# Modulation matmuls of the delta rounds: one weight block of three summed on VectorE

## The chip, the cores and the metric

One core of a Trainium2 chip. The metric is device time of one execution in microseconds (us), the median over runs. All data are float32.

## What is computed

The program is two layers of models behind each other on 256 tokens of width 1024. The first block normalizes the tokens, projects them, runs a short convolution, a gated delta rule (8 heads, both directions), a state-space mixer (SSD), an output projection and an expert layer. The second block runs two attention layers. Each of these scales, shifts and gates its tokens by a modulation vector, which depends on one conditioning row `c` alone:

```python
c_act = jax.nn.silu(c)                        # 1 x 1024
for l in range(DEPTH_2):                      # 2 layers
    mod = c_act @ w_ada[l] + b_ada[l]         # (1 x 1024) @ (1024 x 3072)
    shift, scale, gate = split_cols(mod, (D, D, D))
```

`w_ada` is 2 x 1024 x 3072 floats, 25 MB. It is independent of the tokens, so the kernel computes it while the delta rule runs.

## The kernel before, in words

The kernel is written engine by engine; each engine runs its own list of instructions in the order written, and semaphores order the engines (`Steps` counts named steps of one semaphore, `X.at("name", r)` is its count at that step in round r).

**Weights.** All large weights come through a ring in SBUF, in blocks of 2 MB, in the order of `stream_plan`. The SP queue issues each load as soon as the block that last held the slot has been read. Up to the expert layer only two slots are in use, taken in turn (`n % 2`). The 12 blocks of `w_ada_2` are 1024 x 512: eight row groups k of 128 rows on the partitions, 512 columns each. TensorE takes a block with `take`, and `block_read` puts its release on the next matmul that TensorE issues, whichever it is.

**The delta stage** has four rounds r, two heads (s = 0, 1) in each. A round finishes the inverse of a triangular matrix by block steps and then runs the recurrence. In TensorE's order: P5 (matmuls of `LT` with the operands `Xf` that GpSimd builds), X5 and Y5 (they need G5, the masked P5 that VectorE makes in `masked`), P6, Y6 (needs G6), then the state products u, S, K2, Q2, u2, o. Each is 8 matmul records a head of 128x128 (X5 with Y5 16). VectorE also copies Y5's result to `Y`, ScalarE copies X5's. GpSimd builds the next round's `Xf` and `Yf` as soon as P5 and Y5 of this round no longer read them (four instructions, line 2627).

**The modulation** rides in the same rounds, three blocks n = 3r, 3r+1, 3r+2 each, in two steps:

- `ada_rows(n)`, the row pass: for each k, `ccol[:, k]` (silu of c, 128 values) as weights, widened to 32 columns, and the 128x512 rows of the block as moving operand. Four column strips of bank 6 take k = 0..3 and then k = 4..7 on top, so the bank ends with four partial rows, each in 32 copies. ScalarE (`rows_out`) copies the bank to `ntmp`.
- `ada_cols(n)`: four matmuls with 128x128 pieces of `ntmp` as weights and a column of 1/32 (`one32`) as moving operand; they sum over the partitions and leave the 512 results as four columns in bank 7. VectorE (`ada_out`) copies them to `modc`.

The order in a round before: rows 3r, P5, cols 3r, rows 3r+1, X5 and Y5, cols 3r+1, rows 3r+2, P6, Y6, cols 3r+2, and then the recurrence. Bank 6 is one buffer, so `ada_rows` waits for the ScalarE copy of the block before; bank 7 also, so `ada_cols` waits for VectorE's copy before it.

**Round 0** starts when the gate projection is done and GpSimd has built the first operands from the inverse, which came back through DRAM.

Of the kernel before, what the change touches and what calls it, by code (L numbers as in the profile page):

```python
# [7 lines left out]
P = 128  # L8
F32 = mybir.dt.float32
F32R = mybir.dt.float32r  # L10
ALU = mybir.AluOpType
ACT = mybir.ActivationFunctionType
# [6 lines left out]
DK = D // P  # L19
# [161 lines left out]
def hybrid_kernel(nc, A, out, scratch):  # L181
# [7 lines left out]
    with ctx:  # L189
        def sem(name):  # L190
            return ctx.enter_context(nc.semaphore(name))
# [36 lines left out]
        with ExitStack() as st:  # L228
# [64 lines left out]
            xw = [cT[:, KT0 + 2 * i:KT0 + 2 * i + 2, :].rearrange("p a n -> p (a n)") for i in range(4)]  # L293
            hst = [free[:, (24 + 4 * i) * P:(28 + 4 * i) * P] for i in range(2)]
            yint = late
            onat = knat
            ynat = vnat
            mixT = cT[:, 0:MT, :]
# [181 lines left out]
        ssds_pe = Steps(sem("ssds_pe"), "h y")  # L480
        ssds_pool = Steps(sem("ssds_pool"), "xw")
        ssds_act = Steps(sem("ssds_act"), "h")
        ada_pe = Steps(sem("ada_pe"), "rows cols")
        ada_act = Steps(sem("ada_act"), "rows")
        ada_dve = Steps(sem("ada_dve"), "cols")
        c_ready = sem("c_ready")
        mix_act = Steps(sem("mix_act"), "gdn ssd")
        mix_gdn, mix_ssd = Steps(sem("mix_gdn"), "pair"), Steps(sem("mix_ssd"), "mixed")
        delta_norm = sem("delta_norm")
# [150 lines left out]
        def _(pe):  # L640
# [44 lines left out]
            def mm(o, lhsT, rhs, start=True, stop=True):  # L685
                return release(nc.tensor.matmul(o, lhsT, rhs, start=start, stop=stop))  # L686
# [152 lines left out]
            def ada_rows(n, r):  # L839


                w = take("w_ada_2")
                if n == 0:
                    pe.wait_ge(c_ready, 2)
                if n % 3 == 0 and r:
                    for s in range(2):
                        pe.wait_ge(gdn_act[s].sem, gdn_act[s].at("Q2", r - 1))
                if n:
                    pe.wait_ge(ada_act.sem, n)
                for k in range(DK):  # L850
                    j = k % 4
                    last = mm(bank[6][32 * j:32 * j + 32, :], ccol[:, k:k + 1].to_broadcast([P, 32]), w[:, k, :], k < 4, k >= 4)
                last.then_inc(ada_pe.sem, ada_pe.one("rows"))
                block_read()

            def ada_cols(n):

                pe.wait_ge(ada_act.sem, n + 1)
                if n:
                    pe.wait_ge(ada_dve.sem, n)  # L860
                for i in range(4):
                    last = mm(bank[7][:, i:i + 1], ntmp[:, n % 2, i * P:(i + 1) * P], one32[:])
                last.then_inc(ada_pe.sem, ada_pe.one("cols"))

            def ssd_args(u):

# [10 lines left out]

            pe.wait_ge(lt_pool.sem, GH)
            for r in range(GH // 2):
                ada_rows(3 * r, r)  # L880
                for s in range(2):
                    h = 2 * r + s
                    p_, d_, a_ = gdn_pe[s], gdn_dve[s], gdn_act[s]
# [3 lines left out]
                    for i in range(4):  # L887
                        last = mm(q4(A_[s], i), LT[:, h, i, :], Xf[s][:, i, :])
                    last.then_inc(p_.sem, p_.one("P5"))
                ada_cols(3 * r)  # L890
                ada_rows(3 * r + 1, r)
                for s in range(2):
                    p_, d_, a_ = gdn_pe[s], gdn_dve[s], gdn_act[s]
                    pe.wait_ge(d_.sem, d_.at("G5", r))
                    for i in range(4):
                        last = mm(q4(B_[s], i), Yf[s][:, i, :], G[s][:, i, :])
                    last.then_inc(p_.sem, p_.one("X5"))
                    for i in range(4):
                        last = mm(q4(C_[s], i), G[s][:, i, :], Yf[s][:, i, :])
                    last.then_inc(p_.sem, p_.one("Y5"))  # L900
                ada_cols(3 * r + 1)
                ada_rows(3 * r + 2, r)
                for s in range(2):
# [594 lines left out]
        def _(act):  # L1498
# [8 lines left out]
            def f(o, i, fn, scale=1.0, bias=0.0, **kw):  # L1507
                return nc.scalar.activation(o, i, fn, scale=scale, bias=bias, **kw)  # L1508
# [125 lines left out]
            for r in range(GH // 2):  # L1634
                if r:
                    delta_squares(r - 1)
                def each():
                    for s in range(2):
                        yield s, 2 * r + s, gdn_pe[s], gdn_dve[s], gdn_act[s], gdn_pool[s]
                def rows_out(n):  # L1640
                    act.wait_ge(ada_pe.sem, ada_pe.at("rows", n))
                    f(ntmp[:, n % 2, :], bank[6][:], ACT.Copy).then_inc(ada_act.sem, ada_act.one("rows"))
                rows_out(3 * r)
                rows_out(3 * r + 1)
                for s, h, p_, d_, a_, o_ in each():
                    act.wait_ge(p_.sem, p_.at("X5", r))
                    f(X[s], bank[1 + 3 * s][:].rearrange("p (i n) -> p i n", i=4), ACT.Copy).then_inc(a_.sem, a_.one("X5"))
                rows_out(3 * r + 2)
                for s, h, p_, d_, a_, o_ in each():
                    act.wait_ge(p_.sem, p_.at("Y6", r))  # L1650
                    f(Y[s], bank[2 + 3 * s][:].rearrange("p (i n) -> p i n", i=4), ACT.Copy).then_inc(a_.sem, a_.one("Y6"))
                for s, h, p_, d_, a_, o_ in each():
                    act.wait_ge(d_.sem, d_.at("us", r))
                    f(U[s][:, 0:2, :], bank[6 + s][:, 0:2 * P].rearrange("p (i n) -> p i n", i=2), ACT.Copy
                      ).then_inc(a_.sem, a_.one("u"))
                for s, h, p_, d_, a_, o_ in each():
                    act.wait_ge(p_.sem, p_.at("S", r))
                    f(LT[:, h, 2:4, :], bank[3 * s][:, 0:2 * P].rearrange("p (i n) -> p i n", i=2), ACT.Copy
                      ).then_inc(a_.sem, a_.one("S"))
                for s, h, p_, d_, a_, o_ in each():  # L1660
                    act.wait_ge(p_.sem, p_.at("Q2", r))
                    for i, (c, d) in enumerate(((1, 0), (0, 1))):
                        last = f(QS[s][:, c, :], bank[6 + s][:, i * P:(i + 1) * P], ACT.Copy,
                                 scale=eg[:, c, d * GH + h:d * GH + h + 1])
                    last.then_inc(a_.sem, a_.one("Q2"))
# [314 lines left out]
        def _(dve):  # L1980
# [153 lines left out]
            for r in range(GH // 2):  # L2134
# [4 lines left out]
                    return tt(G[s].rearrange("p (c d) n -> p c (d n)", c=TT), bank[3 * s][:].rearrange("p (c n) -> p c n", c=TT),  # L2139
                              gmask[b].rearrange("p d n -> p (d n)").unsqueeze(1).to_broadcast([P, TT, 2 * P]), ALU.mult)  # L2140
                def ada_out(n):
                    dve.wait_ge(ada_pe.sem, ada_pe.at("cols", n))
                    nc.vector.tensor_copy(modc[:, 4 * n:4 * n + 4], bank[7][:, 0:4]).then_inc(ada_dve.sem, ada_dve.one("cols"))
                for s, h, p_, d_, a_, o_ in each():
                    dve.wait_ge(p_.sem, p_.at("P5", r))
                    masked(s, 5).then_inc(d_.sem, d_.one("G5"))
                ada_out(3 * r)
                for s, h, p_, d_, a_, o_ in each():
                    dve.wait_ge(p_.sem, p_.at("Y5", r))
                    nc.vector.tensor_copy(Y[s], bank[2 + 3 * s][:].rearrange("p (i n) -> p i n", i=4)).then_inc(d_.sem, d_.one("Y5"))  # L2150
                ada_out(3 * r + 1)
                for s, h, p_, d_, a_, o_ in each():
                    dve.wait_ge(p_.sem, p_.at("P6", r))
# [582 lines left out]
```

## Time and profile before

| | |
|---|---|
| median of 3 runs | 1373.17 us (1367.18 to 1374.37) |
| the profiled execution | 1375.73 us |
| its span | 1373.7 us |
| TensorE busy | 1226.6 us (89% of the span) |
| TensorE weight loads, beside it | 926.1 us (67%) |
| VectorE busy | 645.5 us (47%) |
| ScalarE busy | 410.6 us (30%) |
| GpSimd busy | 331.0 us (24%) |

The span is what the profiler saw from the first instruction to the last; the execution's own time is a little longer. A float32 matmul appears as two records. Where an engine is busy 89% over the whole, single stages may still wait for something else, so the shares say little on one stage. The delta stage runs from about 253 to 364 us of the span. "Granted clock" is the share of 2.4 GHz that TensorE was given: 1.00 is 2.4 GHz, 0.50 would be 1.2 GHz, and a value between is a stretch with some of both.

### The profile page before, as it was taken

How to read it: one execution, taken by the hardware profiler on the slowest of the kernel's cores; microseconds unless marked ns; L12 is line 12 of the kernel's file. 1: busy time of each engine (PE TensorE's matmuls, PEld its weight loads, DVE VectorE, ACT ScalarE, POOL GpSimd, SP SyncE). 2: the span in 40 equal slices, each digit the busy share in tenths (PEclk: the TensorE clock that was granted, in tenths of full speed). 3: DMA queues.
4: the chain of work that ended last, by engine and by line, in shares of the span. 5: the costliest groups of instructions: out<-in, count | busy, mean ns of one | idle time of the engine just before them, and what ended most of it. 6: DMA issues, size and time to landing. Idle time of an engine off the chain costs nothing.

```text
span 1373.7 us, 17987 instructions
## 1 busy us (share of the span) xinstructions
PE 1226.6 (89%) x7446; PEld 926.1 (67%) x7446; DVE 645.5 (47%) x1059; ACT 410.6 (30%) x991; POOL 331.0 (24%) x322
## 2 busy tenths in 40 slices
PE   6989789899999699978789998998988999899887
PEld 5878655577754332212129797998878889798777
DVE  1597758133560300001026355575887245466785
ACT  4345542133631410100014521311524441230332
POOL 0386640412200300000021122132253112223231
PEclk9999989999999799999999999999999999999999
DMA  5333333766406699999982435153332245335310
GB/s 196 123 123 123 123 92 134 267 242 218 152 30 275 257 386 421 422 421 422 421 340 71 160 107 204 62 173 134 123 111 85 96 172 170 114 114 184 123 62 31
DMA packets 91554, 257.02 MB, mean 187 GB/s; under 512 B 7645, under 2 KB 12534, under 8 KB 79058
## 3 DMA queue, kind: packets, MB, share of 16 engines
q1 hardware_dynamic: 89122, 248.67, 48.3%
q0 software_dynamic: 2032, 6.95, 1.6%
q8 instruction: 58, 0.95, 0.3%
q10 hardware_dynamic: 320, 0.26, 0.1%
q14 instruction: 22, 0.18, 0.0%
HBM read 253.49 MB, written 2.12 MB: 186 GB/s over the span
## 4 chain that ended last, share of the span: by engine, by line
PE 63%; DMA 14%; DVE 9%; ACT 7%; POOL 5%; issue 2%; SPq 0%; DVEq 0%; ACTq 0%; POOLq 0%
PE bank L686 59%; DMA ring<-in_w_up_dram 8%; DMA ring<-in_w_down_dram 4%; PE bank L695 3%; DVE ring_r L1993 3%; POOL late L2595 3%; POOL acc L2596 2%; DVE acc L2064 2%; ACT ring L1508 1%; DMA ring<-in_w_ada_dram 1%; ACT cT L1508 1%; ACT L1508 1%; ACT oa L1508 1%; ACT qkT L1508 1%; ACT xT L1508 0%
## 5 line engine op out<-in xcount | busy, mean ns | idle before, releaser
L2698 POOL CAST w_hi_r<-ring 128x1024 fp32r<-128x1024 f32 x136 | 151.0, 1138 | 670.4 <-DMA ring<-in_w_in_dram 267.3
L686 PE MATMUL bank<-ring_r,xT_hi 128*128 128x256 f32 (+1 forms) x864 | 245.9, 285 | 0.0
L686 PE MATMUL bank<-w_hi_r,xT_hi 128*128 128x256 f32 x704 | 208.6, 296 | 24.2 <-DVE ring_r L1993 19.8
L686 PE MATMUL bank<-w_hi_r,xT_r 128*128 128x256 f32 x704 | 202.6, 288 | 0.0
L1993 DVE TENSOR_TENSOR ring_r<-ring,w_hi_r 128x1024 fp32r<-128x1024 f32 x136 | 182.6, 1375 | 41.9 <-POOL w_hi_r L2698 41.9
L686 PEld LDWEIGHTS bank<-ring_r,xT_hi 128*128 128x128 f32 x864 | 168.3, 195 | 0.2
L686 PEld LDWEIGHTS bank<-w_hi_r,xT_hi 128*128 128x128 f32 x704 | 137.2, 195 | 36.5 <-DVE ring_r L1993 25.7
L686 PEld LDWEIGHTS bank<-w_hi_r,xT_r 128*128 128x128 f32 x704 | 136.9, 195 | 0.0
L686 PE MATMUL bank<-ring,xsT 128*32 128x512 f32 x496 | 111.8, 595 | 26.4 <-DMA ring<-in_w_up_dram 13.2
L686 PE MATMUL bank<-xT,ring 128*128 128x256 f32 x576 | 127.5, 384 | 0.0
L686 PEld LDWEIGHTS bank<-xT,ring 128*128 128x128 f32 x576 | 111.0, 193 | 15.3
L2064 DVE SCALAR_TENSOR_TENSOR acc<-raw,cols,acc 128x256 f32<-128x256 f32 x168 | 99.3, 600 | 24.2 <-ACT acc L1508 19.3
L686 PEld LDWEIGHTS bank<-ring,xsT 128*32 128x32 f32 x496 | 28.0, 110 | 105.5 <-issue 65.3
L686 PE MATMUL bank<-ring,cT 128*128 128x512 f32 (+1 forms) x224 | 67.7, 460 | 2.8 <-ACT cT L1508 2.8
L2595 POOL TENSOR_SCALAR late<-raw,cols 128x256 f32<-128x256 f32 x48 | 48.6, 1012 | 83.2 <-ACT acc L1508 79.3
L2326 DVE TENSOR_TENSOR hid<-hid,bank 128x512 f32<-128x512 f32 x4 | 2.8, 688 | 134.3 <-PE bank L686 134.3
L1508 ACT ACTIVATE prob<-prob,nmx 128x256 f32<-128x256 f32 x64 | 32.1, 503 | 101.8 <-DVE smx L2451 55.0
L686 PE MATMUL bank<-ring,hidT 128*32 128x512 f32 x256 | 54.7, 595 | 8.0 <-DMA ring<-in_w_down_dram 5.3
L2442 DVE TENSOR_TENSOR prob<-bank,bias 128x256 f32<-128x256 f32 x64 | 24.2, 420 | 77.0 <-PE bank L686 77.0
L1508 ACT ACT_TABLE_LOAD x45 | 57.7, 1283 | 8.5 <-DVE sz L2021 6.1
L686 PE MATMUL bank<-xT_hi,w_hi_r 128*128 128x256 f32 x208 | 59.2, 285 | 0.0
L686 PE MATMUL bank<-xT_hi,ring_r 128*128 128x256 f32 x208 | 58.8, 283 | 0.0
(360 smaller groups left out, 2133.0 us busy)
## 6 DMA issues: line engine op xcount, KB each, us to landing
ring<-in_w_in_dram SPq DMA_DIRECT2D x39, 2048.0 KB, 7.8
ring<-in_w_up_dram SPq DMA_DIRECT2D x32, 1024.0 KB, 16.3
ring<-in_w_down_dram SPq DMA_DIRECT2D x32, 1024.0 KB, 16.3
ring<-in_w_gate_dram SPq DMA_DIRECT2D x30, 1024.0 KB, 16.4
ring<-in_w_ada_dram SPq DMA_DIRECT2D x12, 2048.0 KB, 8.8
ring<-in_w_out_dram SPq DMA_DIRECT2D x8, 2048.0 KB, 7.7
ring<-in_w_o_mla_dram SPq DMA_DIRECT2D x2, 2048.0 KB, 12.6
ring<-in_w_o_swa_dram SPq DMA_DIRECT2D x2, 2048.0 KB, 7.8
```

The source lines that it names most:

```text
L686: return release(nc.tensor.matmul(o, lhsT, rhs, start=start, stop=stop))
L695: return release(nc.tensor.transpose(o, i, eye[0:i.shape[0], 0:i.shape[0]]))
L1508: return nc.scalar.activation(o, i, fn, scale=scale, bias=bias, **kw)
L1993: tt(lo, raw_, hi.bitcast(F32), ALU.subtract).then_inc(lo_done.sem, lo_done.one("piece"))
L2064: ins = stt(out=acc[:, n % 4, :], in0=raw[:, n % 4, j:j + T], scalar=tap(n, j), in1=acc[:, n % 4, :], op0=ALU.mult, op1=ALU.add)
L2326: tt(v, v, bank[1][:], ALU.mult).then_inc(ex_dve.sem, ex_dve.one("h"))
L2442: last = tt(prob[:, u % 2, m, :], bank[m][:, 0:T], bv[:, m, :], ALU.add)
L2595: link(nc.gpsimd.tensor_scalar(prod[:, j % 2], raw[:, n % 4, j:j + T], tap(n, j), None, ALU.mult))
L2596: ins = nc.gpsimd.tensor_tensor(acc[:, n % 4, :], acc[:, n % 4, :], prod[:, j % 2], ALU.add)
L2698: nc.gpsimd.tensor_copy(hi, raw_).then_inc(hi_done.sem, hi_done.one("piece"))
```

## The change

The middle block of each round, 3r+1, is no longer multiplied on TensorE. VectorE (`ada_block`) waits until it has landed and computes the sum over k of `w[:, k] * ccol[:, k]` with one tensor_scalar and seven scalar_tensor_tensor instructions of 128x512, each of which waits for the one before (`link`), into `asum` (a quarter of the `late` buffer). TensorE then sums `asum` over the partitions in `ada_cols(3r+1)`, with a column of ones from `tri`, and takes and releases the block only there. ScalarE's copy for that block is gone.

The order changes too. On TensorE: P5, rows 3r, X5 and Y5, cols 3r, cols 3r+1, rows 3r+2, P6, Y6, cols 3r+2. On VectorE: G5 of both heads, the block sum, both Y5 copies, the copies of cols 3r and 3r+1, G6. The one semaphore for rows and cols becomes two, and `rows_index` counts the remaining row passes.

```diff
@@ -293,6 +293,7 @@
             xw = [cT[:, KT0 + 2 * i:KT0 + 2 * i + 2, :].rearrange("p a n -> p (a n)") for i in range(4)]
             hst = [free[:, (24 + 4 * i) * P:(28 + 4 * i) * P] for i in range(2)]
             yint = late
+            asum = late[3]
             onat = knat
             ynat = vnat
             mixT = cT[:, 0:MT, :]
@@ -480,10 +481,17 @@
         ssds_pe = Steps(sem("ssds_pe"), "h y")
         ssds_pool = Steps(sem("ssds_pool"), "xw")
         ssds_act = Steps(sem("ssds_act"), "h")
-        ada_pe = Steps(sem("ada_pe"), "rows cols")
+        ada_rows_pe, ada_cols_pe = Steps(sem("ada_rows_pe"), "rows"), Steps(sem("ada_cols_pe"), "cols")
+        ada_sum = Steps(sem("ada_sum"), "block")
         ada_act = Steps(sem("ada_act"), "rows")
         ada_dve = Steps(sem("ada_dve"), "cols")
         c_ready = sem("c_ready")
+        n_ada = next(n for n, block in enumerate(plan) if block[0] == "w_ada_2")
+
+        def rows_index(n):
+
+            return n - (n + 1) // 3
+
         mix_act = Steps(sem("mix_act"), "gdn ssd")
         mix_gdn, mix_ssd = Steps(sem("mix_gdn"), "pair"), Steps(sem("mix_ssd"), "mixed")
         delta_norm = sem("delta_norm")
@@ -846,21 +854,29 @@
                     for s in range(2):
                         pe.wait_ge(gdn_act[s].sem, gdn_act[s].at("Q2", r - 1))
                 if n:
-                    pe.wait_ge(ada_act.sem, n)
+                    pe.wait_ge(ada_act.sem, rows_index(n))
                 for k in range(DK):
                     j = k % 4
                     last = mm(bank[6][32 * j:32 * j + 32, :], ccol[:, k:k + 1].to_broadcast([P, 32]), w[:, k, :], k < 4, k >= 4)
-                last.then_inc(ada_pe.sem, ada_pe.one("rows"))
+                last.then_inc(ada_rows_pe.sem, ada_rows_pe.one("rows"))
                 block_read()
 
             def ada_cols(n):
 
-                pe.wait_ge(ada_act.sem, n + 1)
                 if n:
                     pe.wait_ge(ada_dve.sem, n)
+                if n % 3 == 1:
+                    take("w_ada_2")
+                    pe.wait_ge(ada_sum.sem, n // 3 + 1)
+                    v, ones = asum, tri[:, 1, 0:1]
+                else:
+                    pe.wait_ge(ada_act.sem, rows_index(n) + 1)
+                    v, ones = ntmp[:, rows_index(n) % 2], one32[:]
                 for i in range(4):
-                    last = mm(bank[7][:, i:i + 1], ntmp[:, n % 2, i * P:(i + 1) * P], one32[:])
-                last.then_inc(ada_pe.sem, ada_pe.one("cols"))
+                    last = mm(bank[7][:, i:i + 1], v[:, i * P:(i + 1) * P], ones)
+                last.then_inc(ada_cols_pe.sem, ada_cols_pe.one("cols"))
+                if n % 3 == 1:
+                    block_read()
 
             def ssd_args(u):
 
@@ -877,7 +893,6 @@
 
             pe.wait_ge(lt_pool.sem, GH)
             for r in range(GH // 2):
-                ada_rows(3 * r, r)
                 for s in range(2):
                     h = 2 * r + s
                     p_, d_, a_ = gdn_pe[s], gdn_dve[s], gdn_act[s]
@@ -887,8 +902,7 @@
                     for i in range(4):
                         last = mm(q4(A_[s], i), LT[:, h, i, :], Xf[s][:, i, :])
                     last.then_inc(p_.sem, p_.one("P5"))
-                ada_cols(3 * r)
-                ada_rows(3 * r + 1, r)
+                ada_rows(3 * r, r)
                 for s in range(2):
                     p_, d_, a_ = gdn_pe[s], gdn_dve[s], gdn_act[s]
                     pe.wait_ge(d_.sem, d_.at("G5", r))
@@ -898,6 +912,7 @@
                     for i in range(4):
                         last = mm(q4(C_[s], i), G[s][:, i, :], Yf[s][:, i, :])
                     last.then_inc(p_.sem, p_.one("Y5"))
+                ada_cols(3 * r)
                 ada_cols(3 * r + 1)
                 ada_rows(3 * r + 2, r)
                 for s in range(2):
@@ -1638,10 +1653,9 @@
                     for s in range(2):
                         yield s, 2 * r + s, gdn_pe[s], gdn_dve[s], gdn_act[s], gdn_pool[s]
                 def rows_out(n):
-                    act.wait_ge(ada_pe.sem, ada_pe.at("rows", n))
-                    f(ntmp[:, n % 2, :], bank[6][:], ACT.Copy).then_inc(ada_act.sem, ada_act.one("rows"))
+                    act.wait_ge(ada_rows_pe.sem, rows_index(n) + 1)
+                    f(ntmp[:, rows_index(n) % 2, :], bank[6][:], ACT.Copy).then_inc(ada_act.sem, ada_act.one("rows"))
                 rows_out(3 * r)
-                rows_out(3 * r + 1)
                 for s, h, p_, d_, a_, o_ in each():
                     act.wait_ge(p_.sem, p_.at("X5", r))
                     f(X[s], bank[1 + 3 * s][:].rearrange("p (i n) -> p i n", i=4), ACT.Copy).then_inc(a_.sem, a_.one("X5"))
@@ -2139,15 +2153,29 @@
                     return tt(G[s].rearrange("p (c d) n -> p c (d n)", c=TT), bank[3 * s][:].rearrange("p (c n) -> p c n", c=TT),
                               gmask[b].rearrange("p d n -> p (d n)").unsqueeze(1).to_broadcast([P, TT, 2 * P]), ALU.mult)
                 def ada_out(n):
-                    dve.wait_ge(ada_pe.sem, ada_pe.at("cols", n))
+                    dve.wait_ge(ada_cols_pe.sem, n + 1)
                     nc.vector.tensor_copy(modc[:, 4 * n:4 * n + 4], bank[7][:, 0:4]).then_inc(ada_dve.sem, ada_dve.one("cols"))
+                def ada_block(n):
+                    dve.wait_ge(landed[slot[n_ada + n]], arrived(n_ada + n))
+                    dve.wait_ge(c_ready, 2)
+                    w = ring[slot[n_ada + n]][:].rearrange("p (k n) -> p k n", k=DK)
+                    for k in range(DK):
+                        if k:
+                            ins = stt(out=asum, in0=w[:, k], scalar=ccol[:, k:k + 1], in1=asum, op0=ALU.mult, op1=ALU.add)
+                        else:
+                            ins = ts(asum, w[:, k], ccol[:, k:k + 1], None, ALU.mult)
+                        if k < DK - 1:
+                            link(ins)
+                    ins.then_inc(ada_sum.sem, ada_sum.one("block"))
+
                 for s, h, p_, d_, a_, o_ in each():
                     dve.wait_ge(p_.sem, p_.at("P5", r))
                     masked(s, 5).then_inc(d_.sem, d_.one("G5"))
-                ada_out(3 * r)
+                ada_block(3 * r + 1)
                 for s, h, p_, d_, a_, o_ in each():
                     dve.wait_ge(p_.sem, p_.at("Y5", r))
                     nc.vector.tensor_copy(Y[s], bank[2 + 3 * s][:].rearrange("p (i n) -> p i n", i=4)).then_inc(d_.sem, d_.one("Y5"))
+                ada_out(3 * r)
                 ada_out(3 * r + 1)
                 for s, h, p_, d_, a_, o_ in each():
                     dve.wait_ge(p_.sem, p_.at("P6", r))
```

## Rows read from the trace of the kernel before

**Rows 1.** Chain that ended last, shares of the span by engine.

```profile
PE 63%; DMA 14%; DVE 9%; ACT 7%; POOL 5%; issue 2%; SPq 0%; DVEq 0%; ACTq 0%; POOLq 0%
```

**Rows 2.** Stretches: length, busy PE, PEld, DVE, ACT, POOL; clock, DMA share, GB/s.

```profile
253.00:279.00 26.00, 21.03 (x162) 15.56 (x163) 6.59 (x15) 4.74 (x9) 9.93 (x8) 0.93 0.88 311
279.00:304.00 25.00, 24.57 (x208) 19.64 (x207) 8.01 (x19) 8.00 (x23) 5.03 (x4) 1.00 0.67 239
```

**Rows 3.** Chain in order of time, its transfers of 225 to 400 us.

```profile
254.57 7.78 DMA ring<-in_w_ada_dram
...
338.75 8.78 DMA ring<-in_w_ada_dram
```

**Rows 4.** Timeline of round 1, TensorE: start, length, instruction, count.

```profile
285.05 1.92 PE L686 MATMUL bank<-ring,ccol 128*32 128x512 f32 x16
...
286.90 2.05 PE L686 MATMUL bank<-ring 128*128 128x128 f32 x16
...
288.79 0.95 PE L686 MATMUL bank<-one,ntmp 128*128 128x1 f32 x8
...
291.52 3.84 PE L686 MATMUL bank<-ring 128*128 128x128 f32 x32
...
297.93 3.99 PE L686 MATMUL bank<-cT,ring 128*128 128x128 f32 x32
```

**Rows 5.** The same timeline, VectorE: last sum of round 0, G5, Y5 copy.

```profile
285.15 0.42 DVE L2176 TENSOR_TENSOR w_hi<-bank,ring 128x256 f32<-128x256 f32 x1 [0.47 <-PE bank L686]
...
288.99 0.69 DVE L2139 TENSOR_TENSOR ring<-bank,tri 128x512 f32<-128x512 f32 x1 [0.20 <-PE bank L686]
...
293.61 0.69 DVE L2150 COPY cT<-bank 128x512 f32<-128x512 f32 x1 [3.67 <-PE bank L686]
```

**Rows 6.** VectorE by line (ns min/median/max), and the convolution from 52 us.

```profile
L2565 DVE SCALAR_TENSOR_TENSOR xres<-tmp,stat,xres x4: 745/748/752, 1035.5 to 1359.0; 128x512 f32<-128x512 f32 x4
...
L1997 DVE CAST xT_hi<-xT 128x512 fp32r<-128x512 f32 x8 | 3.4, 425 | 7.1 <-ACT xT L1508 7.1
...
L2064 DVE SCALAR_TENSOR_TENSOR acc<-raw,cols,acc x168: 470/486/1011, 52.1 to 181.5; 128x256 f32<-128x256 f32 x168
...
52.06 5.91 DVE L2064 SCALAR_TENSOR_TENSOR acc<-raw,cols,acc 128x256 f32<-128x256 f32 x9
...
52.00:58.00 6.00, 6.00 (x29) 5.29 (x28) 5.72 (x10) 1.79 (x4) 5.45 (x7) 1.00 0.34 102
```

**Rows 7.** Timeline: GpSimd in round 1, GpSimd and VectorE from 363 us.

```profile
293.66 3.75 POOL L2627 TENSOR_TENSOR ring<-cT,tri 128x512 f32<-128x512 f32 x3 [4.24 <-PE bank L686]
...
363.52 4.62 POOL L2647 TENSOR_TENSOR w_hi<-xnat,drow 128x1024 f32<-128x1024 f32 x2 [3.57 <-DVE w_hi L2176]
...
365.41 0.97 DVE L2210 TENSOR_TENSOR cT<-cT 128x512 f32<-128x512 f32 x1 [1.33 <-ACT cT L1508]
...
367.47 1.22 DVE L2192 TENSOR_TENSOR ring<-ring 128x512 f32<-128x512 f32 x1 [1.09 <-ACT ring L1508]
```

**Rows 8.** Load of block 5: its issue, and KB with us to landing.

```profile
287.42 0.37 SPq L621 DMA_DIRECT2D ring<-in_w_ada_dram  x1
...
ring<-in_w_ada_dram SPq DMA_DIRECT2D x1, 2048.0 KB, 7.9
```

**Rows 9.** Round 0: TensorE's timeline, and the stretch 262 to 265.

```profile
253.52 1.92 PE L686 MATMUL bank<-ring,ccol 128*32 128x512 f32 x16 [0.84 <-issue]
...
256.70 1.16 PE L686 MATMUL bank<-ring 128*128 128x128 f32 x8 [1.25 <-POOL ring L2627]
...
259.16 1.16 PE L686 MATMUL bank<-ring 128*128 128x128 f32 x8 [1.30 <-POOL ring L2627]
...
264.80 4.89 PE L686 MATMUL bank<-ring 128*128 128x128 f32 x32
...
272.26 4.00 PE L686 MATMUL bank<-cT,ring 128*128 128x128 f32 x32
...
262.00:265.00 3.00, 2.61 (x17) 0.62 (x18) 0.00 (x0) 0.09 (x1) 0.00 (x0) 0.77 1.05 388
```

## The prediction, made before the changed kernel was run

> **What bounds the kernel now.** I read the page first. The chain that ended last is TensorE for 63% and transfers for 14% [rows 1], so work taken from another engine is worth nothing unless TensorE waits for it. Then I cut the delta stage into its rounds. From the second round on TensorE is busy 24.57 of 25 us at full clock, VectorE only 8.01 [rows 2]: the stage is TensorE's instruction order, one round every 25.67 us (P6 starts at 272.26 in round 0 and at 297.93 in round 1) [rows 4, 9]. In round 0 it is not: TensorE is busy 21.03 of 26 us at clock 0.93. The chain of waits adds one thing [rows 3]: two transfers of modulation blocks are on it, 7.78 us in round 0 and 8.78 us in round 3. So the third block of a round lands about when TensorE wants it: the two-slot ring has next to no slack today, which a moved release will show.
>
> **One round in TensorE's order** [rows 4], offsets from 285.05: row pass of block 3 at 0.0, P5 1.85, column sums 3.74, row pass of block 4 4.62, X5 and Y5 6.47, column sums 10.15, row pass of block 5 11.03, P6 12.88 (of the row passes and column sums, which repeat, the first stands in the rows). Back to back, a row pass takes 1.85 us, column sums 0.88, P5 1.85, X5 with Y5 3.68. VectorE's mask G5 of the second head ends 2.78 us after P5 starts (288.99 + 0.69 against 286.90) [rows 4, 5].
>
> **What the change removes.** One row pass a round, 1.85 us of TensorE, and one ScalarE copy, which lay beside TensorE's work and was worth nothing. Without new waits P6 would start at 11.0 instead of 12.88. Moving the other row pass behind P5 costs nothing by itself in rounds 1 to 3: P5 then needs bank 0 and 3 free, and VectorE's last sum of the round before starts at 285.15 and takes 0.42 us [rows 5], done while the first head's P5 (about 1 us) runs.
>
> **What it adds on VectorE.** One tensor_scalar and seven scalar_tensor_tensor, 128x512, chained. The row with the same form (a per-partition scalar, both tensors in SBUF) is 748 ns; the one-source op of that size, a cast, 425 ns [rows 6]. With 0.04 us for each link (the chained 128x256 ops run 486 ns) that is 0.43 + 7 x 0.75 + 8 x 0.04 = 6.0 us, undisturbed.
>
> They will be disturbed. GpSimd builds the next round's operands as soon as Y5 of the first head is done: three instructions of 1.25 us, now from 293.66, 2.1 us after X5 starts [rows 7]. In the new order X5 starts at 3.7, GpSimd at about 5.8, in the middle of the block sum (2.8 to 8.8). Two rows bound what that does. VectorE ops of 0.69 us with both inputs in SBUF took 0.97 and 1.22 us when they started just before a GpSimd instruction ended: they waited it out [rows 7]. If three ops each wait for a whole instruction, the sum is 6.0 + 3 x 1.25 = 9.8 us. In the convolution, with GpSimd nearly always busy, nine chained ops took 5.91 us, 0.66 each instead of 0.53 (486 ns and a link) [rows 6]: a quarter more, so by that row only 6.0 + a quarter of 3.75 = 6.9 us. There nine ops got through beside seven GpSimd instructions [rows 6], so an instruction does not always block from end to end. These operands are larger (128x512 and two inputs), nearer to the first row; I take 0.8 us per GpSimd instruction, 8.4 us in all.
>
> The Trainium skill has a rule here: SBUF — State Buffer, section Who interferes with whom, says that a VectorE instruction with two SBUF inputs and a GpSimd instruction that reads SBUF exclude each other for the whole instruction. The 0.97 and 1.22 us agree with it, the convolution's 0.66 us does not; by the rule the block sum is the 9.8 us above.
>
> **The new wait.** The block sum sits ahead of VectorE's two Y5 copies (0.69 us each [rows 5], 1.3 together) and the small copy of the first column sums (1.5 with that and the handover), and TensorE's second column sums wait for both the block sum and that copy, since bank 7 is shared. All TensorE work of the round is queued behind: the third row pass, P6, Y6 and the recurrence. So P6 starts at 2.8 (G5) + D + 1.5 + 0.88 + 1.85 = D + 7.03. With D = 8.4 that is 15.4, 2.55 us later than now; with 6.9 it is 13.9; with 9.8 it is 16.8, 3.95 later. ScalarE's X5 copies are not behind the sum. Break-even for this wait is D = 5.85.
>
> **The transfers.** A slot is released by the next matmul behind the one that read it. Block 3r+2 goes to block 3r's slot, until now asked for behind the first row pass (SP issued it at 287.42, 2.37 us into the round) and landed 7.9 us later; alone, such loads take 7.8 to 8.8 us [rows 8]. Now its slot is released at X5's first matmul, 3.7 us in, and issued 0.52 us later (as 287.42 behind 286.90). It lands at 4.2 + 7.9 = 12.1, so P6 cannot start before 14.0, 1.1 us later than now (2.0 with 8.8). This floor holds however fast VectorE is. At D = 8.4 it is hidden under VectorE's wait. The other block of the round is held until its column sums and has 15 us and more before the next use: free.
>
> **Round 0** is worse. Its blocks come from the idle stretch in front, where TensorE waits for GpSimd's first operands. Block 0 was read at 253.52, before P5; now it waits for P5, whose second head ends at 260.3, and its 1.85 us are no longer hidden [rows 9]. Block 1's slot was released by the row pass at 253.52 (issued 254.57 [rows 3]); now by P5 at 256.70, issued 257.22, landing near 265.1. X5 can start at 262.2. VectorE starts the sum at 265.1; about 8.0 us (GpSimd overlaps less), then 1.5 + 0.88 + 1.85, puts P6 at 277.3. Today P6 starts at 272.26 [rows 9]: 5.1 us. With 6.0 us it is 3.1, with 9.8 us (from 265.5) 7.3.
>
> **Sum.** 5.1 + 3 x 2.55 = 12.8 us. Behind the stage nothing absorbs it: the chain runs on without a fixed date, the expert loads wait for a semaphore of the SSD stage, which moves along. Waits of 4 to 7 us also open in front of TensorE. In round 0 today, after a stretch half idle, its clock was 0.77 of full, so in part at 1.2 instead of 2.4 GHz, and X5 with Y5 took 4.89 instead of 3.84 us [rows 4, 9]: 1.05 us, and with the row pass before them, at the same ratio, about 1.6. I put 1 us in for the four rounds. The profiled execution took 1375.73 us (its span 1373.7), so its own forecast is 1389.5; the runs' median is 2.6 us lower, 1373.17, and the prediction stands against that: 1387.
>
> **Rivals.**
> *The transfer alone sets the pace.* GpSimd disturbs little, D is 6 to 7, P6 starts at 14.0: 3.1 + 3 x 1.1 = +6.4 us, 1379.6. For it: the convolution row. Against: the two ops that waited. Chance 0.17.
> *Full exclusion, and a fallen clock.* D = 9.8: 7.3 + 3 x 3.95 = +19.2 us, 1392; if the clock also drops behind every wait as in round 0, 4 x 1.6 more, 1399. By the Trainium skill, TensorE: Matmul & The Clock Gate, section HAM oscillation, waits between bursts of matmuls put the clock back to half; rows 9 agree, while rounds 1 to 3, which hardly wait now, show 1.00. Chance 0.24.
> *Not slower: the row pass is really gained.* At the second column sums; it decides if D is under 5.85 and block 3r+2 lands in under 6.8 us. At its fullest (D = 4.0, eight ops at the cast's rate) 3 x 1.85 = 5.6 us less and round 0 even: 1367.6. Against: 748 ns for the form, and no load of this size under 7.8 us. Chance 0.05.
> *The delay is absorbed later,* by a stage waiting for something with its own date: 1373. I find none. Chance 0.04.
> *My forecast* (VectorE's sum is the wait, GpSimd partly in its way): 0.50.
>
> **How the numbers follow.** A measurement of this kernel tells about 0.5%, 6.9 us, from no change. Slower by more: 0.50 + 0.24 and half of the transfer case, which lies at that bound, 0.83. Within: the rest of it, the absorbed case and most of the gained one, 0.15. Faster: 0.02, since even the full gain is 5.6 us. The range goes from a little under the transfer case to the full exclusion with some of the clock: 1378 to 1397.
>
> **What the profile will show.** Each round has eight chained VectorE ops with a mean near 0.9 to 1.1 us against 0.75; the slow ones are those beside GpSimd. TensorE has a gap of 3 to 5 us between two column sums in every round, ended by VectorE, or a second short one ended by a modulation transfer if VectorE was faster. Periods of rounds 1 to 3 near 28.2 us (26.8 if the transfer sets them), state products of round 0 some 5 us later. Clock 1.00 in rounds 1 to 3 would take the clock out. I am wrong if the period stays at 25.7 or falls, if VectorE's sum is under 6 us, or if the stage grows and the whole does not.

## The result

| | before | after |
|---|---|---|
| median | 1373.77 us (1367.18 to 1376.47, 4 runs) | 1397.73 us (1394.08 to 1401.05, 4 runs) |
| profiled execution | 1375.73 us, span 1373.7 | 1401.05 us, span 1399.2 |
| granted clock over the span | 0.971 | 0.956 |

The ratio is 1.0164, with a 95% interval of 1.0143 to 1.0186: slower, by 24 us between the two medians (22.5 us by the ratio) where 14 were forecast. The median of 1397.73 us lies 0.7 us above the upper end of the range; the ratio, put on the 1373.17 us that the forecast started from, gives 1395.7 us, just inside it.

The head of the page after, busy times and the chain that ended last:

```profile
span 1399.2 us, 17888 instructions
...
PE 1234.4 (88%) x7382; PEld 932.9 (67%) x7382; DVE 674.2 (48%) x1091; ACT 408.1 (29%) x987; POOL 333.0 (24%) x322
...
PE 57%; DMA 14%; DVE 14%; ACT 6%; issue 4%; POOL 4%; SPq 0%; DVEq 0%; POOLq 0%; ACTq 0%
```

Two things stand in it. VectorE's share of the chain rose from 9% [rows 1] to 14%, so TensorE now waits for it. And TensorE, with four row passes of 1.85 us less to do, is busy 1234.4 us instead of 1226.6: it does less work in more time. The mean granted clock fell with it, and the lines below show where.

Round 1 of the delta stage after (it answers to [rows 4, 5, 7]); start, length, engine, line, instruction, count, and in brackets the idle time in front with what ended it:

```profile
296.74 1.92 PE L694 MATMUL bank<-ring,ccol 128*32 128x512 f32 x16
296.84 0.69 DVE L2153 TENSOR_TENSOR ring<-bank,tri 128x512 f32<-128x512 f32 x1 [0.20 <-PE bank L694]
297.45 0.48 DVE L2166 TENSOR_SCALAR late<-ring,ccol 128x512 f32<-128x512 f32 x1
297.96 8.14 DVE L2164 SCALAR_TENSOR_TENSOR late<-ring,ccol,late 128x512 f32<-128x512 f32 x7
298.59 3.84 PE L694 MATMUL bank<-ring 128*128 128x128 f32 x32
...
300.72 4.83 POOL L2655 TENSOR_TENSOR ring<-cT,tri 128x512 f32<-128x512 f32 x3 [3.44 <-PE bank L694]
302.26 0.95 PE L694 MATMUL bank<-one,ntmp 128*128 128x1 f32 x8
...
306.02 1.28 DVE L2177 COPY cT<-bank 128x512 f32<-128x512 f32 x2
307.42 1.87 PE L694 MATMUL bank<-tri,late 128*128 128x1 f32 x8 [4.21 <-DVE modc L2157]
309.22 3.64 PE L694 MATMUL bank<-ring,ccol 128*32 128x512 f32 x16
312.79 4.36 PE L694 MATMUL bank<-cT,ring 128*128 128x128 f32 x32
...
318.28 1.13 PE L694 MATMUL bank<-w_hi,cT 128*128 128x128 f32 x8 [0.35 <-DVE modc L2157]
```

Read it down TensorE's lines. The row pass in front of X5 takes 1.92 us, X5 with Y5 3.84, the first column sums 0.95: full speed. Then TensorE is idle for 4.21 us, until VectorE has finished the block sum, the two Y5 copies and the small copy. Behind the gap the same column sums take 1.87 us and the same row pass 3.64. The granted clock of that stretch says the same (length, busy PE, PEld, DVE, ACT, POOL; clock, DMA share, GB/s), in round 0 and in round 1:

```profile
276.00:283.00 7.00, 6.81 (x31) 3.82 (x32) 0.30 (x3) 0.60 (x1) 0.00 (x0) 0.51 0.27 71
283.00:307.00 24.00, 19.53 (x163) 17.22 (x162) 16.19 (x27) 7.05 (x21) 6.12 (x4) 0.99 0.67 243
307.00:314.00 7.00, 6.58 (x31) 3.59 (x32) 0.53 (x3) 0.60 (x1) 0.00 (x0) 0.53 0.24 54
```

For nearly 7 us behind each of these two gaps TensorE has 1.2 GHz, and 2.4 GHz again after it (the 7 us behind the gap of round 2 show 0.55). The chain of the same stretch, in order of time, shows both causes in a row: VectorE's chained operations of 1.65 us, then one long stretch of TensorE.

```profile
300.32 0.76 DVE late L2164
...
302.79 1.65 DVE late L2164
...
304.46 1.64 DVE late L2164
306.10 1.20 DVE cT L2177 x2
...
307.42 10.53 PE bank L694 x64
```

The measure used from here on is the start of a round's first state product (`bank<-w_hi,cT`, the last line of the timeline above), and the period from one round to the next; for round 0 it is the time since its first P5. Spans differ by some us in the stages in front from one execution to the next, periods do not carry that.

| | P5 to state product, round 0 | period, round 1 | 2 | 3 |
|---|---|---|---|---|
| before | 20.7 | 25.67 | 25.67 | 25.83 |
| after | 29.9 | 30.98 | 30.86 | 29.73 |
| longer by | 9.2 | 5.3 | 5.2 | 3.9 |

With 0.7 us by which the stage begins later (P5 at 257.40 instead of 256.70) that is 24.3 of the 25.5 us between the two spans. The other 1.2 us are not placed. Nothing is absorbed behind the stage.

### The profile page after: what moved, and what is told of

Read it like the earlier page. It is cut to its first block, busy times and chain, and to the rows that moved or that the text cites. A ratio compares the mean times of both kernels' runs of the same rounds, so it can differ in the third digit from the quotient of the medians.

```text
span 1399.2 us, 17888 instructions
## 1 busy us (share of the span) xinstructions
PE 1234.4 (88%) x7382; PEld 932.9 (67%) x7382; DVE 674.2 (48%) x1091; ACT 408.1 (29%) x987; POOL 333.0 (24%) x322
## 4 chain that ended last, share of the span: by engine, by line
PE 57%; DMA 14%; DVE 14%; ACT 6%; issue 4%; POOL 4%; SPq 0%; DVEq 0%; POOLq 0%; ACTq 0%
PE bank L694 55%; DMA ring<-in_w_up_dram 8%; DMA ring<-in_w_down_dram 4%; DVE acc L2078 3%; DVE ring_r L2007 3%; PE bank L703 3%; DVE late L2164 2%; POOL late L2623 1%; ACT ring L1523 1%; DMA ring<-in_w_ada_dram 1%; POOL acc L2624 1%; ACT cT L1523 1%; ACT L1523 1%; DVE ring L2091 1%; DMA inverses<-late 1%
## 5 line engine op out<-in xcount | busy, mean ns | idle before, releaser
L694 PEld LDWEIGHTS bank<-w_hi_r,xT_hi 128*128 128x128 f32 x704 | 137.4, 195 | 36.5 <-DVE ring_r L2007 25.7
```

## The experiments

Forecast was a wait of 2.55 us a round with a clock that hardly matters; 5.3 came. The runs below take the wait and the clock apart, then GpSimd's part, then the transfer's; the last four move the work to other places. All times are medians, all ratios are against the kernel before on the same chip, whose median was 1375.91 us in runs 1 to 4, 1377.04 us in 5 and 6 and 1375.34 us in 7. So kernels of different sections are compared by their ratios. The lines come from one execution of each kernel: in run 2 and run 4 that was the slowest one (1394.26 and 1391.39 us), in run 5 the fastest (1394.27 us).

### 1. Keep TensorE busy in the gap

```diff
 def ada_cols(n):
+    if n % 3 == 1:
+        for _ in range((16, 9, 9, 2)[n // 3]):
+            nc.tensor.matmul(bank[0][:, 0:256], eye[:], tri[:, 0:2, :].rearrange("p a n -> p (a n)"), start=True, stop=True)
     if n:
         pe.wait_ge(ada_dve.sem, n)
```

> The changed kernel with extra matmuls (results unused) on TensorE in the gap before the second column sums: 16 of 128x256 in round 0, 9 in rounds 1 and 2, 2 in round 3. Theory A (the clock fell to half for about 6 to 7 us behind each gap because TensorE stood still, worth about 3 us a round): the row pass behind the gap takes 1.9 instead of 3.6 us, the granted clock stays near 1.00, each of rounds 0 to 2 gets 2.5 to 3 us shorter, 1389 us in all. Rival B (these matmuls are slow for another cause, such as the operands that VectorE just wrote): nothing changes or it gets slower, 1397 to 1400 us.

Measured: 1387.13 us (1386.52 to 1387.52, 4 runs), ratio 1.0084 [1.0054, 1.0113]. Round 1, TensorE, and then the windows view of the stretch behind the gap:

```profile
296.20 4.13 PE L868 MATMUL bank<-tri,eye 128*128 128x256 f32 x18
300.56 1.05 PE L694 MATMUL bank<-tri,late 128*128 128x1 f32 x8 [0.23 <-DVE modc L2160]
301.55 1.92 PE L694 MATMUL bank<-ring,ccol 128*32 128x512 f32 x16
303.40 4.00 PE L694 MATMUL bank<-cT,ring 128*128 128x128 f32 x32
```

```profile
300.00:307.00 7.00, 6.76 (x56) 4.91 (x55) 2.06 (x5) 1.06 (x2) 0.00 (x0) 1.00 0.45 141
```

The wait for VectorE is still there, only filled with useless matmuls, and the work behind it runs at full clock. Periods are 28.11, 28.10 and 28.35 us, so of the 5.3 us in round 1, 2.9 (30.98 - 28.11) were the clock and 2.4 (28.11 - 25.67) the wait, and in round 2 nearly the same. The forecast for the wait alone was 28.2. In round 3 the transfer of the third block still makes TensorE wait for 1.22 us, and the row pass behind it takes 3.35 us. Doing 36 more matmuls makes the changed kernel about 11 us faster (1.0084 against 1.0164; 1389 us were expected).

### 2. GpSimd out of VectorE's way

```diff
+if r and s == 0:
+    pool.wait_ge(ada_sum.sem, r)
```

ahead of GpSimd's build of the next round's operands.

> The changed kernel, but GpSimd builds the next round's operands only when VectorE's block sum is done. Theory A (each GpSimd instruction delays one chained VectorE operation by about 0.9 us, three in a round, so 2.7 us): the block sum takes 6.0 us in all rounds instead of 8.65. Then the next transfer becomes the wait, as in round 3 already: the period of rounds 1 and 2 falls from 30.9 to about 29.7, not to 28.2; 1394 us. Rival B (VectorE's wait alone sets the period, transfers have slack): 28.2 us a round, 1390 us. Rival C (the longer operations have another cause than GpSimd): no change, 1398 us.

Measured: 1389.51 us (1386.86 to 1394.26), ratio 1.0105 [1.0069, 1.0141]. VectorE's sum by form here and, below it, in the kernel after; each line has busy time, mean of one and idle time:

```profile
L2164 DVE SCALAR_TENSOR_TENSOR late<-ring,ccol,late 128x512 f32<-128x512 f32 x28 | 21.1, 752 | 1.0
```

```profile
L2164 DVE SCALAR_TENSOR_TENSOR late<-ring,ccol,late 128x512 f32<-128x512 f32 x28 | 28.2, 1005 | 1.0
```

Undisturbed each operation takes 752 ns (748 were taken from [rows 6]). In the kernel after, the source view gives 750 minimum, 752 median and 1655 maximum: most are not touched at all. The extra time comes in steps of 0.9 us, three a round in rounds 0 to 2, as many as there are GpSimd instructions beside the sum (in round 0 one of the three hits the first operation, which takes 1.30 us instead of 0.48). That is 7.1 us in these lines and 0.8 in the first operation of round 0. Yet the rounds do not fall to the price of the wait that is left, since TensorE now meets another one:

```profile
301.45 1.05 PE L694 MATMUL bank<-tri,late 128*128 128x1 f32 x8 [1.55 <-DVE modc L2157]
...
304.10 3.64 PE L694 MATMUL bank<-ring,ccol 128*32 128x512 f32 x16 [1.59 <-DMA ring<-in_w_ada_dram]
```

Block 3r+2 has not landed, and the clock has fallen behind this second wait (1.59 us in round 1, 1.29 and 1.28 in the next two, each with 1.5 us for VectorE before it): periods 29.86, 28.43 and 29.58. Round 1 came as expectation A had it (29.7), round 2 lies nearer to rival B's 28.2, and 1389.51 us is B's total, though the transfer wait that B ruled out is there.

### 3. Both

The edits of 1 (with 11, 4, 4 and 2 matmuls) and 2 together.

> Both edits: GpSimd later, and fillers of 11, 4, 4 and 2 matmuls in the gaps. Theory A (clock and GpSimd are two terms, the transfer the floor under them): rounds 1 to 3 at about 26.8 us, the transfer's floor of 1.1 us over the kernel before, 1382 to 1384 us in all. Rival B (the clock term comes back because TensorE still waits for the transfer): 28 to 29 us a round, 1388 us.

Measured: 1385.24 us (1381.31 to 1388.52, 7 runs), ratio 1.0065 [1.0042, 1.0087]; periods 28.94, 26.97, 29.83. The row passes of rounds 1, 2 and 3 in TensorE's timeline:

```profile
298.63 3.58 PE L694 MATMUL bank<-ring,ccol 128*32 128x512 f32 x16 [1.77 <-DMA ring<-in_w_ada_dram]
...
327.26 1.92 PE L694 MATMUL bank<-ring,ccol 128*32 128x512 f32 x16 [1.45 <-DMA ring<-in_w_ada_dram]
...
354.25 3.64 PE L694 MATMUL bank<-ring,ccol 128*32 128x512 f32 x16 [1.50 <-DMA ring<-in_w_ada_dram]
```

In all three the modulation transfer is last. In round 2 the clock held, and the period is 26.97 us: the floor that the prediction worked out for the transfer was 26.8 (25.7 + 1.1). In the other two the row pass behind a wait of 1.77 us, and of 1.50 us with 0.57 us for VectorE before it, took nearly twice as long, as at half the clock. So A's 26.8 us came in one round of three, and its 1382 to 1384 us were missed.

### 4. Nearly no VectorE work

```diff
-for k in range(DK):
+for k in range(1):
```

VectorE does one of the eight operations, without the link behind it; the output leaves out seven eighths of the middle blocks' products.

> The changed kernel with only the first of the eight VectorE operations of each block sum; seven eighths of the middle blocks' product are left out. What stays is the new order and the moved releases. Theory A (the transfer of the third block is a floor of its own: it is asked for only behind X5's first matmul): TensorE now waits 2 to 3 us for that transfer in each round, P6 starts 14.0 us into the round against 12.88 before; 1380 us if the clock holds, up to 1388 us if it falls in this gap too. Rival B (only VectorE's sum made the change slow): rounds of 24 to 25.7 us, 1369 to 1373 us.

Measured: 1386.95 us (1383.36 to 1391.39, 6 runs), ratio 1.0074 [1.0048, 1.01]; periods 29.51, 28.30, 29.64. Round 1, TensorE, and the two steps of the chain there:

```profile
297.71 1.05 PE L694 MATMUL bank<-tri,late 128*128 128x1 f32 x8 [0.26 <-DVE modc L2157]
301.27 3.64 PE L694 MATMUL bank<-ring,ccol 128*32 128x512 f32 x16 [2.51 <-DMA ring<-in_w_ada_dram]
```

```profile
293.35 7.88 DMA ring<-in_w_ada_dram
...
301.27 9.45 PE bank L694 x56
```

With VectorE's sum as good as gone, the row pass taken from TensorE is still not gained: each round is 2.6 to 3.8 us longer than before. The load of block 3r+2, 7.88 us long, is asked for only when X5 starts, and TensorE stands 2.51 us for it. Of the 3.8 us of round 1 the transfer itself is about 1.0, as the prediction's floor has it (1.1); the other 2.8 are the clock, 1.72 in the row pass and 1.08 in P6 and Y6 (5.07 us instead of 3.99). So with this slot released only at X5's first matmul, the change would be slower even with a VectorE that cost nothing.

### 5. The row pass 3r back in front of P5, nothing else

```diff
 for r in range(GH // 2):
+    ada_rows(3 * r, r)
     ...
-    ada_rows(3 * r, r)
```

> The changed kernel with one part undone: the row pass of block 3r is back in front of P5. Theory A (its move cost round 0 some 4 us, because the row pass had filled an idle stretch and released a slot early, but in rounds 1 and 2 it had covered VectorE's sum): round 0 about 4 us shorter, P5 at full clock; rounds 1 and 2 about 1.9 us longer, 32.5 to 33 us, since VectorE starts the sum 1.85 us later in the round; 1396 to 1399 us. Rival B (the moved release of block 3r's slot was what bound rounds 1 and 2): they get shorter, 1385 us.

Measured: 1398.33 us (1394.27 to 1399.76, 4 runs), ratio 1.0162 [1.0131, 1.0192]. Its first P5, and its gap in round 1:

```profile
249.96 1.16 PE L694 MATMUL bank<-ring 128*128 128x128 f32 x8
...
299.10 1.87 PE L694 MATMUL bank<-tri,late 128*128 128x1 f32 x8 [6.10 <-DVE modc L2157]
```

Round 0 gets better: 27.0 us from P5 to the state product instead of 29.9, since the pass again lies in TensorE's idle stretch and P5 finds the full clock (1.16 us, where it is 2.04 in the kernel after; in runs 1 and 3, with the order of the kernel after, it took 1.13, so this part isn't due to the order alone). Rounds 1 and 2 get worse, 33.49 and 34.50 us: less TensorE work now lies beside the block sum, and the gap is 6.10 us instead of 4.21, in round 2 7.43. There the sum takes 9.95 us: two more GpSimd instructions lie beside it, and two more of its operations are slowed, to 1.42 us each. Round 3 takes 30.62 us instead of 29.73. The medians show no change (1.0162 and 1.0164), though the four rounds of this execution add up to 4.1 us more than in the kernel after; its stage begins 7.4 us earlier, and the runs don't tell which part of that belongs to the edit.

### 6. Column sums out of VectorE's way

In the next two the block sum is cut in two parts (five operations behind G5, three behind G6), the middle block's column sums move behind Y6 beside those of the third block, with one copy for both, and the third row pass lies between P6 and Y6. A slot that VectorE reads is released by VectorE's own count:

```diff
+if plan[n][0] == "w_ada_2" and (n - n_ada) % 3 == 1:
+    return ada_sum.sem, (n - n_ada) // 3 + 1
```

> The middle block still on VectorE, but off TensorE's path: row pass 3r stays in front of P5 and its column sums behind P5; the column sums of block 3r+1 move behind Y6, beside those of 3r+2; P6 comes before the third row pass; VectorE does five operations behind G5 and three behind G6; VectorE itself releases the block; GpSimd builds its operands after the sum. Theory A (the removed row pass is worth its 1.85 us once nothing on TensorE waits for VectorE or for a late release): rounds of 23.6 to 24.2 us at full clock, 1363 to 1368 us. Rival B (another wait takes its place, of a block whose slot is now released later, or of Y6 for G6 behind the sum): rounds of 25.7 us and more, 1373 us or above.

> As the kernel with late column sums, but GpSimd builds its operands as early as before, beside VectorE's sum. Theory A (the longer operations, 2 to 2.7 us a round, now have slack in front of the late column sums, but the Y5 copies and G6 stand between them): within 1 us a round of the other, 1363 to 1371 us. Rival B (VectorE's operations set the path again): 2 us or more a round slower than the other.

Measured, with GpSimd held back until the sum is done: 1372.33 us (12 runs), ratio 0.9964 [0.9947, 0.9982], periods 24.85, 25.20, 25.11. With GpSimd as early as in the kernel before: 1374.12 us (12 runs), ratio 0.9981 [0.9964, 0.9999], periods 25.96, 26.87, 24.20. In front of the column sums TensorE's wait for VectorE is gone in rounds 1 to 3 of the first, and 0.71 and 0.18 us in rounds 1 and 2 of the second. Both are slower than was expected (1363 to 1368 and 1363 to 1371 us), and faster than the kernel before by less than 0.4%. Compared with each other, the means of the twelve runs differ by 2.6 us, with an interval from 0.1 to 5.1, so GpSimd as early as before costs something here, and the runs hardly settle how much. What is left is the transfer, here in the first of them, round 2; the second line stands 5.4 us behind the end of that row pass:

```profile
321.15 1.92 PE L696 MATMUL bank<-ring,ccol 128*32 128x512 f32 x16 [1.47 <-DMA ring<-in_w_ada_dram]
...
328.47 2.07 PE L696 MATMUL bank<-ring,w_hi 128*128 128x128 f32 x8 [0.26 <-DVE ring L2191]
```

The row pass has the full clock, but the state product there takes 2.07 us instead of 1.23, and the stretch from 328 to 333 us shows 0.66. Round 0 waits longest for its transfer (2.32 us) and its row pass takes 2.95 us.

### 7. The third row pass at the end as well

```diff
                 last.then_inc(p_.sem, p_.one("Y6"))
+            taken[0] += 1
+            ada_rows(3 * r + 2, r)
+            ada_cols(3 * r + 1)
             ada_cols(3 * r + 2)
```

Row pass 3r is in front of P5 again, the column sums of 3r behind P6, and VectorE does four operations behind G5 and four behind G6. GpSimd is held back.

> As the kernel with late column sums, but the third row pass moves behind Y6 too, and the column sums of block 3r go between P6 and Y6. Theory A (in the kernel with late column sums each round still waits up to 2.3 us for the transfer of the third block, 7.9 to 9.2 us behind its release; TensorE now asks for it some 2 us later): no wait for that transfer in rounds 1 to 3, rounds of 23.8 to 24.2 us at clock 1.00, 3 to 4 us less than the kernel with late column sums, 1367 to 1370 us against about 1377 before. Rival B (G6 or the loads of the next round become late instead): rounds of 25 us and more, 1372 us.

Measured: 1368.04 us (1363.81 to 1368.92, 6 runs) against 1375.34 for the kernel before (11 runs), ratio 0.9935 [0.9911, 0.9959]. Round 2, TensorE, and the windows view of that round:

```profile
316.38 1.95 PE L696 MATMUL bank<-cT,ring 128*128 128x128 f32 x16
318.16 0.95 PE L696 MATMUL bank<-one,ntmp 128*128 128x1 f32 x8
318.97 2.03 PE L696 MATMUL bank<-cT,ring 128*128 128x128 f32 x16
320.94 1.92 PE L696 MATMUL bank<-ring,ccol 128*32 128x512 f32 x16
322.79 1.05 PE L696 MATMUL bank<-tri,late 128*128 128x1 f32 x8
...
325.08 1.13 PE L696 MATMUL bank<-w_hi,cT 128*128 128x128 f32 x8 [0.35 <-DVE modc L2160]
```

```profile
302.00:326.00 24.00, 23.31 (x196) 19.53 (x194) 14.07 (x29) 7.65 (x22) 5.11 (x5) 1.00 0.75 265
```

No wait stands in front of the row pass or the column sums, the clock is 1.00, and VectorE is busy 14 of 24 us, while TensorE waits for it only as it did before (0.35 us for the small copy). Periods are 24.74, 23.83 and 23.83 us. In rounds 2 and 3 of this run that is 25.67 - 1.84, the whole of the row pass that was taken from TensorE; round 1 begins with 6.5 us at clock 0.74, whose cause no run isolates. This kernel beats both.

## Why the prediction was off where it was

**What bounds the kernel, the new place of the wait: right.** The gap is where it was put, between the two column sums, ended by VectorE's small copy; 4.21 us long in round 1 and 4.22 in round 2 (3 to 5 forecast for every round; it was 7.67 in round 0 and 1.54 in round 3).

**The block sum: right within 0.3 us in rounds 1 and 2.** In round 1 it takes 8.65 us (297.45 to 306.10) where 8.4 were taken. Its parts: a first operation of 0.48 us, undisturbed ones of 0.75 (as taken), and three of 1.65. So the price comes to 0.9 us for each GpSimd instruction; 0.8 was taken, between the bounds of 0.3 and 1.25. By the Trainium skill, SBUF — State Buffer, section Who interferes with whom, the two exclude each other for the whole instruction, which would be the 1.25; the runs bear out that there is a price for each instruction, but not all of it. That GpSimd pays too (4.83 us for the three instead of 3.75 [rows 7]) was not in the sum, and cost nothing.

**The wait: right in rounds 1 and 2, too long in round 3.** In rounds 1 and 2 28.1 us were measured with the clock held, 28.2 forecast. In round 3 GpSimd has no next round's operands to build, the sum takes 5.9 us and not 8.4, and the term should have been the transfer floor of 1.1 us and not 2.55. The prediction put GpSimd's price on all three rounds.

**The transfer floor: right.** Runs 3 and 4 show it once VectorE is quick enough, 26.97 us against 26.8. It also sets round 3 of the changed kernel: TensorE first waits 1.54 us for VectorE and then for the block. (Of the two transfers that the prediction read off the chain, the one of round 0 is the round's second block, wanted by the row pass at 262.39; only the one of round 3 is a third block.)

```profile
366.60 1.05 PE L694 MATMUL bank<-tri,late 128*128 128x1 f32 x8 [1.54 <-DVE modc L2157]
...
369.04 3.64 PE L694 MATMUL bank<-ring,ccol 128*32 128x512 f32 x16 [1.38 <-DMA ring<-in_w_ada_dram]
372.61 5.13 PE L694 MATMUL bank<-cT,ring 128*128 128x128 f32 x32
```

The last two lines are 1.72 and 1.14 us longer than at full clock, together 2.9 of that round's 3.9 us; the 1.0 left is the floor.

**Round 0: 9.2 us where 5.1 were forecast.** Its rows in the kernel after:

```profile
257.40 2.04 PE L694 MATMUL bank<-ring 128*128 128x128 f32 x8 [4.08 <-POOL ring L2655]
...
266.29 1.30 DVE L2166 TENSOR_SCALAR late<-ring,ccol 128x512 f32<-128x512 f32 x1 [3.72 <-DMA ring<-in_w_ada_dram]
267.62 7.25 DVE L2164 SCALAR_TENSOR_TENSOR late<-ring,ccol,late 128x512 f32<-128x512 f32 x7
...
276.19 1.87 PE L694 MATMUL bank<-tri,late 128*128 128x1 f32 x8 [7.67 <-DVE modc L2157]
277.99 3.64 PE L694 MATMUL bank<-ring,ccol 128*32 128x512 f32 x16
```

The steps came in the order given. The sum begins at 266.29 (265.8 by the forecast, moved by the 0.7 us of the later P5) and takes 8.6 us instead of 8.0: the column sums start 0.9 us later than worked out. The other 3.3 us are the clock, 0.92 in the column sums, 1.72 in the row pass and the rest in P6 and Y6.

**The step that failed is the clock term.** "I put 1 us in for the four rounds" was read from round 0 of the kernel before, at 0.77 of full, and put in as if it were that round's alone. It should have been a term of every round with a gap: 3.3 us in round 0 and 2.9 in each of the others, together about 12, half of the measured 24.3. Without it the forecast was 12.8, and what is left is 12.3, 0.7 of it from in front of the stage. That these agree so well is in part luck: round 0 has 5.9 us where 5.1 were forecast, round 3 has 1.0 where 2.55 were, and the two misses pull against each other. The 12 us are partly worked out from the lengths of instructions; run 1 shows 2.9 and 2.8 in rounds 1 and 2 directly, and 2.6 in round 0 (27.3 us from P5 to the state product instead of 29.9). The rival with a fallen clock had the mechanism right, with 4 x 1.6 us for it, but tied it to a block sum of 9.8 us, which did not come. By the Trainium skill, TensorE: Matmul & The Clock Gate, section HAM oscillation, waits between bursts of matmuls put the clock back to half: this trace agrees, with 0.51 and 0.53 behind the gaps, and the prediction cited it but priced it only in the rival.

**What stays open.** Why a wait of 1.45 us left the clock alone in round 2 of run 3, while those of the other rounds of run 3 did not, and why in round 2 of run 6 the row pass behind 1.47 us had the full clock and a product some us later had not; no run here tells that. Whether round 3's 3.9 us are split as given was not tried by itself. The 24.74 us of round 1 in run 7 stay open too.

## What to carry to other kernels

Work taken off the bound engine is gained only where the replacement's result is wanted late enough: put the sum, the copy and the column sums behind everything that doesn't need them, and the 1.84 us a round come in full (rounds 2 and 3 of run 7). A new gap in front of TensorE has two prices, its length and the slow stretch behind it (here 4.21 us idle, of which 2.4 were lost, and 2.9 more at 1.2 GHz), so put a price on the clock at each gap, and read it from the lengths of the instructions behind it. A release of a ring slot that moves with the work it rides on is a wait of its own: here it made rounds 2.6 to 3.8 us longer when VectorE had next to nothing to do, about 1.0 us by the wait itself and the rest by the clock behind it.

## What the runs showed of the hardware

- TensorE's clock fell from 2.4 to 1.2 GHz behind a single idle time of 1.77 us (run 3, round 1), and behind shorter ones with another wait some us before: 0.57 and 1.22 us (run 1, round 3), 0.57 and 1.50 (run 3, round 3), 1.54 and 1.28 (run 2, round 3). It stayed at 2.4 GHz behind 1.45 us (run 3, round 2). This is what these rounds show, and no more is read from it. A 128x512 row pass then takes 3.64 us instead of 1.92, four column sums 1.87 instead of 0.95.
- Useless matmuls in the gap were worth about 11 us of 1397.7 (ratio 1.0084 instead of 1.0164).
- A VectorE operation with both inputs in SBUF (128x512) takes 752 ns alone and 1.65 us where a GpSimd instruction of 1.25 us runs beside it; the GpSimd instructions grow from 1.25 to 1.6 us. In rounds 0 to 2 of the kernel after, as many VectorE operations pay as there are GpSimd instructions beside the sum, and the others stay at 0.75.
